# A two-layer decoder trunk on one core: the flag test moved behind all one-hot products, and the attention's maxima, exponentials and low parts in another order

## The reference

```
qkv = h @ w_qkv                       # 16 query heads, 2 key/value heads of 64
q = rms_norm(q, q_gain) * 64 ** -0.5 ; k = rms_norm(k, k_gain)
s = q k^T - slope * dist              # window of 128, in blocks of 128 queries x 256 keys
m = max(max(s), sink)
p = exp(s - m) ; p = p / (sum(p) + exp(sink - m))
o = p v ;  x = x + o @ w_out          # then the experts of layer 1
```

## Time and the profile before

| what | us |
|---|---|
| median of 3 runs | 846.54 (843.29 to 849.91) |
| profiled execution | 846.49 |
| its span | 844.7 |
| PE busy | 790.1 (94%) |
| DVE busy | 601.6 (71%) |
| ACT busy | 465.9 (55%) |
| POOL busy | 160.1 (19%) |

### The profile page before, as it was taken

How to read it: one execution, slowest core, us unless ns; L and a number is a source line. 1 busy time by engine, 2 the same in 40 slices (tenths; PEclk the granted TensorE clock), 3 DMA queues, 4 the chain that set the end, 5 groups by cost and what they waited for, 6 DMA issues and landing times.

```text
span 844.7 us, 11098 instructions
## 1 busy us (share of the span) xinstructions
PE 790.1 (94%) x4236; PEld 554.8 (66%) x4236; DVE 601.6 (71%) x821; ACT 465.9 (55%) x633; POOL 160.1 (19%) x169
## 2 busy tenths in 40 slices
PE   5999999999999899998998999999899899999992
PEld 3454545555688778776876554656579778777771
DVE  3699974766654888887995465666745798897890
ACT  5043202814333387877893227677635488687781
POOL 4400002400001222322210001133101223323121
PEclk9999999999999899999999999999999899999997
DMA  9422020204552499999986100042063699999852
GB/s 368 161 83 86 16 100 1 100 1 150 211 212 102 178 419 359 317 314 330 316 291 258 81 0 1 18 182 100 1 272 126 231 403 349 309 319 334 313 176 34
DMA packets 31451, 160.94 MB, mean 191 GB/s; under 512 B 7601, under 2 KB 7729, under 8 KB 16032
## 3 DMA queue, kind: packets, MB, share of 16 engines
q1 hardware_dynamic: 18432, 130.03, 40.5%
q0 software_dynamic: 11232, 24.60, 10.4%
q10 hardware_dynamic: 1728, 5.52, 1.8%
HBM read 152.32 MB, written 24.12 MB: 209 GB/s over the span
## 4 chain that ended last, share of the span: by engine, by line
PE 54%; DMA 22%; DVE 12%; ACT 6%; POOL 2%; issue 2%; DVEq 0%; ACTq 0%; SPq 0%; POOLq 0%
DMA ring<-stream 21%; PE PS L1789 11%; PE PS L1976 9%; PE PS L2225 8%; DVE w_lo L988 7%; PE PS L1755 3%; PE PS L2106 3%; ACT w_hi L686 3%; PE PS L2260 2%; PE PS L2131 2%; PE PS L1921 2%; PE PS L2273 2%; PE PS L2283 1%; PE PS L2006 1%; PE PS L2039 1%
## 5 line engine op out<-in xcount | busy, mean ns | idle before, releaser
L988 DVE TENSOR_TENSOR w_lo<-ring,w_hi 128x2048 fp32r<-128x2048 f32 x92 | 209.9, 2289 | 41.8 <-ACT w_hi L686 38.6
L686 ACT ACTIVATE w_hi<-ring 128x2048 fp32r<-128x2048 f32 x86 | 164.7, 1917 | 49.6 <-DMA ring<-stream 44.6
L2106 PE MATMUL PS<-w_hi,left_hi 128*128 128x512 f32 x512 | 174.4, 402 | 8.1 <-DVE w_lo L988 5.8
L2106 PEld LDWEIGHTS PS<-w_hi,left_hi 128*128 128x128 f32 x512 | 96.1, 188 | 31.9 <-DVE w_lo L988 5.5
L2106 PE MATMUL PS<-w_lo,left_hi 128*128 128x512 f32 x256 | 100.2, 391 | 0.0
L2131 PE MATMUL PS<-w_hi,left_lo 128*128 128x512 f32 x256 | 85.5, 394 | 7.8 <-DVE left_lo L988 6.7
L2225 PE MATMUL PS<-ring,hT 128*128 128x512 f32 (+1 forms) x192 | 74.3, 532 | 0.0
L536 POOL DMA_INDIRECT arena<-rows x32 | 43.3, 1352 | 118.3 <-PE PS L2083 106.1
L2131 PEld LDWEIGHTS PS<-w_hi,left_lo 128*128 128x128 f32 x256 | 48.0, 188 | 20.9 <-DVE left_lo L988 9.4
L1789 PE MATMUL PS<-ring,hT 128*128 128x512 f32 x128 | 57.6, 599 | 0.4 <-ACT arena L732 0.4
L1789 PE MATMUL PS<-hT,ring 128*128 128x512 f32 x128 | 56.3, 595 | 0.0
(11 more groups left out here) (274 smaller groups left out, 1365.4 us busy)
## 6 DMA issues: line engine op xcount, KB each, us to landing
ring<-stream SPq DMA_DIRECT2D x110, 1024.0 KB, 16.4
arena<-stream SPq DMA_DIRECT2D x6, 1024.0 KB, 8.3
rows<-arena POOLq DMA_DIRECT2D x8, 512.0 KB, 3.1
x<-stream SPq DMA_DIRECT2D x4, 1024.0 KB, 6.5
x<-x_in SPq DMA_DIRECT2D x4, 512.0 KB, 5.3
x<-x_in ACTq DMA_DIRECT2D x4, 512.0 KB, 4.3
sums<-x POOLq DMA_DIRECT2D x4, 512.0 KB, 3.8
x<-sums SPq DMA_DIRECT2D x4, 512.0 KB, 4.7
```

The costliest lines, as they stand in the source:

```text
L686: act.activation(w_hi[pair], held_slot(layer, m), ACT.Copy).then_inc(w_hi_done, 1)
L988: return V.tensor_tensor(out, a, b, op)
L2106: ins = mm(PS[:, gate_bank(e), :], a, b, start=k == 0 and t == 0, stop=k == KD - 1 and t == 2)
```

## The change

The flag test: PE does spread for the fourth tile together with the others, ahead of the test; before, the test stood between the third and the fourth tile, and the transposes of tile 0 between the fourth tile's two halves. The loop behind the flag does all four tiles again, where it did three.

The attention: in block 0 of the loop, most of the second unit comes ahead of normed_heads on DVE. Behind the loop, most(6) comes ahead of biased(7, 0), summed(6) and attended(5) ahead of most(7); normed_odd(6) moves from DVE to ACT; attended(6), a low part, comes ahead of two additions. ACT does exps(7) in halves with copies between them. PE does attend(6) ahead of turn_probs(7, 0) and out_first(3, front) ahead of turn_probs(7, 1).

```diff
-            return 14 if u == 7 else 2 * u + 1
+            return 2 * u + 1
         def sum_inverted(u):
-            return 15 if u == 6 else 2 * u + 2
+            return 2 * u + 2
...
-            def exps(u):
+            def exps(u, heads=range(8)):
                 pr = probs[u % 2]
-                act.wait_ge(m_done, most_done(u))
-                for h in range(8):
+                if 0 in heads:
+                    act.wait_ge(m_done, most_done(u))
+                for h in heads:
                     act.activation(pr[:, h, :], pr[:, h, :], ACT.Exp, bias=am[u % 2][:, h:h + 1],
                                    accum_out=aes[u % 2][:, h:h + 1])
-                act.activation(ane[u % 2], ane[u % 2], ACT.Exp).then_inc(p_exp, 1)
+                if 7 in heads:
+                    act.activation(ane[u % 2], ane[u % 2], ACT.Exp).then_inc(p_exp, 1)
...
             attended_hi(5)
-            exps(7)
+            normed_odd(6)
+            exps(7, range(4))
             turned_probs(6, 0)
+            exps(7, range(4, 8))
             turned_probs(6, 1)
+            attended_hi(6)
             turned_probs(7, 0)
-            attended_hi(6)
             turned_probs(7, 1)
...
                     attended(a - 1)
-                normed_heads(n + 1)
-                most(b)
+                    normed_heads(n + 1)
+                    most(b)
+                else:
+                    most(b)
+                    normed_heads(n + 1)
...
             biased(6, 1)
+            most(6)
             biased(7, 0)
-            most(6)
             biased(7, 1)
+            summed(6)
+            attended(5)
             most(7)
-            summed(6)
-            normed_odd(6)
-            attended(5)
             summed(7)
             normed_odd(7)
+            attended(6)
             add(1, 0, 0)
             add(1, 0, 1)
-            attended(6)
             add(1, 0, 2)
...
                     if layer == 0:
-                        for tt in range(TT - 1):
-                            for j in range(2):
+                        for tt in range(TT):
+                            for j in (1, 0) if tt == TT - 1 else (0, 1):
                                 ins = spread(j, tt)
...
                 spread(1, tt).then_inc(last_psum, 1)
+            spread(1, TT - 1)
+            spread(0, TT - 1).then_inc(last_psum, 1)
             experts_over(0)
-            spread(1, TT - 1)
             turn_tile(1, 0)
-            spread(0, TT - 1).then_inc(last_psum, 1)
...
             out_second(2, back)
-            turn_probs(7, 0)
             attend(6, 0)
             attend(6, 1)
+            turn_probs(7, 0)
+            out_first(3, front)
             turn_probs(7, 1)
-            out_first(3, front)
             attend(7, 0)
```

## The result

| | median us | runs |
|---|---|---|
| before | 847.80 | 6 (843.29 to 850.23) |
| changed | 841.88 | 6 (837.74 to 842.95) |

The ratio of changed to before is 0.9937, 95% interval 0.9908 to 0.9966. That is 5.3 us less, with bounds of 2.9 and 7.8 (the two medians are 5.9 us apart). The forecast was 841.3. The profiled execution took 840.95 us, its span 839.3 against 844.7. Timed once more later, beside the kernel before at 845.71 (13 runs), the changed kernel had 841.87 (8 runs, ratio 0.9954, 0.9937 to 0.9971; 3.9 us less), so I take the gain as 4 to 5 us.

A forecast was written before the change was run, and what follows sets the result against it. PE, with 54% of the chain of waits, was taken to bound the kernel, almost alone between the two layers' experts. 0.4 + 2.8 + 2.0 = 5.2 us off 846.5 gave 841.3 us, range 838.0 to 845.8.

The forecast's parts named there:

- The one distance that I had named in advance: From the first projection to out_second(3): 154.3 us before, should be 149.5 to 150.4.
- The flag test: PE at layer 0's flag test: all eight products ahead of the branch win 0.4 us, ends -0.9 and +3.5.
- the gap starts only when the products end: PE's stall at the flag test: new products hide none of its 3.12 us, hence only +0.4.
- a gap of about 3 us: Sign of being right at the flag test: 32 products in a row, then this gap and half clock behind.
- The second rival: Stall at the flag test goes or is hidden: 1.8 to 4.8 us, in place of 0.4; chance 0.10.
- Block 1: Attention's second block: maxima in DVE's idle time bring scores 1.1 us earlier; no half clock saves 1.7 us more.
- the rival: Half clock stays in block 1 and comes in the tail: only 1.6 us won, 844.9 us; chance 0.23.
- The tail: Attention's last units: reordered work starts out_second(3) at 617.4 instead of 619.40, 2.0 us won, ends 0.4 and 2.6.
- the one of 0.8: PE wait of 0.8 us expected at 616.6 in the tail, beside five of 0.3 to 0.6.
- The third rival: In the tail, exps(6) starts at 596.8 as before, delaying most(7): 2.0 us slower, 848.5 us; chance 0.05.
- I carry the gains over one to one: Time won before 618 us reaches the end in full, since late weights and ring transfers start earlier by it.

The follow-up runs named there:

- earlier test: Changed kernel with PE's flag test of layer 0 moved ahead of all one-hot products, directly behind the last expert's products: 839.44 us, ratio to before 0.9926.
- maxima alone: Kernel before with only most(1) moved ahead of normed_heads(1) in block 1: 843.58 us, ratio 0.9971.
- maxima and tail: Changed kernel with the flag test's edit undone, so both attention edits remain: 840.29 us, ratio to before 0.9951.
- products twice: Changed kernel with the fourth tile's eight one-hot products done twice ahead of the flag test: 840.84 us in one run.
- before, again: Kernel before, unchanged, run once more for a second profile: 844.3 us.
- fillers at the router: Changed kernel with twelve transposes of a constant ahead of each of layer 1's last two tiles' router products: 842.59 us, ratio to before 0.9972.
- tail alone: Kernel before with only the edits of the attention's tail: 843.27 us, ratio 0.9981.
- changed, again: Changed kernel, unaltered, run once more for a second trace: 841.87 us.

## Why the prediction came out right, step by step

**The total** was 0.6 us off, which is in part luck: one term was too large for most executions, one loss was not in the sum, and one gain lies ahead of all edits. The base was luck too. I took 846.5 us for the kernel before; in the later sessions its medians were 844.90 to 845.85 (13 to 31 runs), and 1.6 us of the profiled execution was a fall of the clock that its second trace doesn't have. The one distance that I had named in advance, from the first projection to out_second(3), fell from 154.3 to 150.3 us (462.11 to 612.44), inside the 149.5 to 150.4 of the forecast, though 1.3 us of it is the longer projection.

**The flag test**, forecast +0.4. PE does 32 products in a row and then stalls, and the half clock moves onto the projection, as described; column A falls from a mean of 20.5 (five traces of the old order) to 19.6 (the five with the eight products ahead once). So +0.9, but with 17.9 to 22.0 among those five, so that a gain is likely and not shown. The step that failed is "the gap starts only when the products end", with the stall at its full 3.12 us. The signs given for it, "a gap of about 3 us", came true in one trace of five; the others have 2.0 to 2.4. The second rival was therefore partly at work, with 0.9 of the 3.5 to 4 us that I gave it. The earlier test shows about its whole size, 1.9 to 2.1 us on average.

**Block 1**, forecast 1.1 + 1.7. The first is 1.13 (maxima alone against the second trace of before) to 1.48 (with the tail edit, 146.81 to 145.33). The second is not tied to this wait: three of the four traces with the wait have full clock behind it. This is a step that failed, hidden by the execution it was taken from: I had the row that warned of it, 1.84 us of idle with full clock behind the earlier trace rows, gave the rival 0.23, and reasoned that less idle time must help.

**The tail**, forecast 2.0. B falls by 2.24 when the tail edit comes alone (149.05 to 146.81) and by 2.59 on top of the maxima (147.92 to 145.33); the upper bound given was 2.6. The order in my schedule was met: most(7) behind summed(6), exps(7) in halves, DVE's odd heads of unit 7 ahead of attended(6). The small waits are there, five of 0.28 to 0.64 us from 589 to 612, without the one of 0.8, and the clock stays at 1.00. The clock's part of this term holds up better than in block 1: all four traces without the tail edit have a wait of 2.77 to 2.80 us and half clock behind it, and none of the nine with it has half clock in the tail. The third rival, the tail turning round, asked for exps(6) to start 4.2 us late, in the idle time's place of before; it starts at 588.08, right behind ACT's copies, as in the schedule.

**"I carry the gains over one to one"** failed in stage C. Behind SP's three ring transfers nothing in the code was changed, but C takes 45.4 to 46.0 us in the four traces without the tail edit (mean 45.7) and 45.9 to 47.7 in the eight with it and without fillers (mean 46.6). 0.9 us goes there on average, 1.87 in the profiled execution. The place is in the timelines, before and then changed:

```profile
651.13 3.65 PE L2006 MATMUL PS<-param,arena 128*128 128x20 f32 x32
654.63 2.42 PE L2039 MATMUL PS<-const 128*128 128x128 f32 x12
```

```profile
644.17 5.86 PE L2012 MATMUL PS<-param,arena 128*128 128x20 f32 x32
649.87 2.80 PE L2045 MATMUL PS<-const 128*128 128x128 f32 x12
```

The last 32 router products start 28.7 us after the three ring transfers in both, and take 5.86 us instead of 3.65. Before, the half clock came at 655 to 658.5, over the kernel's own fillers (the products on constants, which nobody waits for), and again at 661.5; it cost little. Now it comes at 645, over products that the routing waits for. The twelve traces without fillers sort by this without an exception. Where the fall starts 32.3 to 32.8 us after the ring transfers, behind the router products, C is 45.4 to 46.0: the four without the tail edit, and two with it ("maxima and tail", "products twice"). Where it starts 29.5 to 31.2 us after them, C is 46.5 to 47.7: the other six with the tail edit. So the loss is shown to be half clock over the router products. That the tail edit brings the fall forward is a correlation, six traces of eight against none of four; why it falls there at all, with PE busy 4.00 of 4.00 us on both sides of 645, is open, and the fillers could not settle it.

**The start** of layer 0's one-hot products is 450.6 to 451.2 in the eight traces with an attention edit and without the early test, and 451.6 to 451.7 in the three traces without an attention edit. That is 0.4 to 1.1 us ahead of every changed instruction that is executed; it is in all of these sums, and it can't be a gain of the edits' work. It arises between SP's late weights at 220 us and those at 292 (71.7 to 72.2 us apart in the three traces, 70.2 to 71.3 in the eight). Layer 0's router lies there, and here too a fall of the clock meets the last 32 router products at another point in each execution ("before, again", then "products twice"):

```profile
273.22 5.58 PE L2006 MATMUL PS<-param,arena 128*128 128x20 f32 x32
```

```profile
274.26 3.66 PE L2012 MATMUL PS<-param,arena 128*128 128x20 f32 x32
```

They take 3.66 to 5.58 us. The two shortest (3.66, 3.70) belong to the two earliest starts and the two longest (5.54, 5.58) to two of the three latest. The kernel before (4.68, with the latest start of the eleven) doesn't fit in as well, so this is part of the cause and perhaps not all. It also says that such a fall moves over router products without any edit ahead of it, which weakens the tie between layer 1's fall and the tail edit further.

## What to carry to other kernels

A stretch of half clock that follows a wait in one trace is not a property of the wait: look at a second execution of the same kernel before crediting it to an edit, and credit only the shorter way. When idle time is taken out of one stage, ask where the next fall of the clock lands, on filler work or on a product that something waits for. PE's branch over a long body cost 2 to 3.6 us here, with the products around it in either order. Directly behind the last expert's products, ahead of a wait, it cost 0.4 to 0.9 us: try another place for such a branch before rearranging what surrounds it. And what an execution wins ahead of the first changed instruction is not the change's.

## What the runs showed of the hardware that I had not expected

Idle time and clock: full clock behind waits of 2.71, 1.84 and (three times of four) 1.66 us, half clock behind 1.67 us once and behind 2.77 to 2.80 in the tail; behind the 2.05 us stall of one and the same order half clock once ("changed") and full clock once ("fillers at the router"); half clock also at 645 us with PE busy throughout. The lengths of the idle times alone do not sort these.

The half clock at the test lasts 3.5 to 4 us in eight traces and 7 us in two ("tail alone", "changed, again"), in the latter with the projection at 9.17 us. In three there is none: the two with the early test, and "fillers at the router".

The stall at a taken branch varies by 1.6 us between two executions of one program (2.05 and 3.63), more than the whole flag edit is worth.
